# Weight strips taken in pairs: matmuls that alternate between two PSUM banks, instead of 24 in a row into one

## The chip, the cores and the metric

The kernel runs on one core of a Trainium2 chip. The metric is the device time of one execution in microseconds; the shown time is the median of three runs.

## The reference, cut to what matters

Two small networks run one after the other on 512 tokens of width 1024, all in float32. The first has two layers: a state-space mixer with a gated output (`w_glu`), an MLP of 4096, a gated per-layer embedding, then keys and values, sliding-window attention, a second MLP and a second gate. The second has a retention and convolution layer and a latent-attention layer. Nearly all of the work is products of the 512 token columns with weight matrices:

```
ab = y @ w_glu
h = h + jnp.square(jax.nn.relu(hm @ w_up[i])) @ w_down[i]
gate = jax.nn.sigmoid(rmsnorm(h, norm_ple[i]) @ w_ple_gate[i])
hk = rmsnorm(h, kv_norm);  hk @ w_k;  hk @ w_v
mix = swa_sink_attention(q, k_shared, v_shared, attn_sinks[j]) @ w_o[j]
return (o.reshape(b, s, MLA_V) * jax.nn.silu(gate)) @ w_out
```

Each of these lines is a phase (or several) of the common loop that the change touches.

## The kernel before, in words

Tokens lie along the free axis (512 columns), features on the 128 partitions in 8 tiles. Weights arrive as 288 **strips** of 128 x 1024 float32, one strip for each 128 output features with its eight 128x128 blocks (k = 0 to 7). The strips go in one fixed order, the list `PHASES`: `proj0` 2, `glu` 16, the MLP phases `up0_c` and `down0_c` (8 each, eight phases, in the order up 0, up 1, down 0, up 2, down 1, up 3, down 2, down 3), `gate0` 8, `kv` 4, `q` 8, `wo` 8, `proj1` 2, the same MLP phases of layer 1, `gate1` 8, `even` 56, `eout` 16, `odd` 6, `qb` 6, `kvb` 4, `mgate` 8, `oout` 8.

A strip passes four stages, through a ring of `RING = 4` slots:

- SyncE loads it into `raw` (`next_strip`, L394) once the slot's last strip has its low part.
- ScalarE rounds it to `whi` (`split_strip`, L498). It does so for the strip three ahead (`LEAD`) of strip l once `seg_done` says that strip l - 1 is finished, since its slot is then free. `ahead` and `ahead_loop` are these calls, and they stand between ScalarE's other work in program order.
- GpSimd makes the rest `wlo = raw - whi` (`low_strip`, L465) and increments `lo_ready`.
- TensorE multiplies. The token operand too is kept as a high and a low part (`Ah`, `Al` and so on), and a product is three matmuls: whi x high, whi x low, wlo x high (`product`, L831 to L833). So a strip is 8 x 3 = 24 matmuls that accumulate in one PSUM bank; strip l uses bank l modulo 4. Before it starts, `strip` waits for `lo_ready` of the strip and for `evac`, which says that the bank's last result has been read. In the first strip of a phase it also waits for each token tile's `x_lo`.

VectorE and ScalarE read the bank (`evac`), apply the root-mean-square scale, activation or addition, and write the next tiles' high (ScalarE, L521) and low (VectorE, L1375) parts.

`strips` (L933 on) is the common loop: phases without `between` run as a hardware loop of four strips a turn. Five phases (`up0_0`, `gate0`, `kv`, `up1_0`, `gate1`) have `between=norm`: after strip 0 TensorE multiplies the sum of squares with a matrix of ones (`norm`, L949) into another bank, ScalarE takes the root (`root`, L527), VectorE the reciprocal (L1391), and no result of the phase can be read before that. In `mlp` and in the `kv` phase ScalarE's `root` stands ahead of the split of the phase's strip 3 in its program; in `gate` the split of strip 3 stands ahead of `root`, and each later split behind the sigmoid (L637) of one tile.

The phases `proj`, `q`, `even`, `eout`, `odd`, `qb`, `kvb` and `mgate` use other functions (`short_strip`, `strip` alone, `strip_part`) or loops of their own, and stay as they are: 108 of the 288 strips. In `eout` two strips in a row, one from `A` and one from `C`, accumulate into the same bank.

Of the kernel before, what the change touches and what calls it, by code (L numbers as in the profile page):

```python
# [14 lines left out]
P = 128  # L15
TOK = 512
D = 1024
KT = D // P
# [26 lines left out]
RING = 4  # L45
# [14 lines left out]
S0, SEG0, OUT0, NSTR, SEGS = {}, {}, {}, {}, {}  # L60
# [41 lines left out]
class Chain:  # L102
# [14 lines left out]
    def each(self, i, per):  # L117
        self.at, self.first = (i, per), self.n
# [6 lines left out]
def program(nc, a):  # L125

    with ExitStack() as top:
        def sem(name):
            return top.enter_context(nc.semaphore(name))

        def area(stack, name, shape, dt=F32):
            return stack.enter_context(nc.sbuf_tensor(name, shape, dt))


        ps = top.enter_context(nc.psum_tensor("ps", [P, 8, 512], F32))
# [37 lines left out]
        whi = area(main, "whi", [P, RING, D], FR)  # L173
        wlo = area(main, "wlo", [P, RING, D], FR)
        with ExitStack() as p0:
            X = {"P": tuple(area(p0, "P" + part, [P, 2, TOK], FR) for part in "hl")}
# [64 lines left out]
        lo_ready = sem("lo_ready")  # L241
        seg_done = sem("seg_done")
        evac = sem("evac")
        x_hi = sem("x_hi")
        x_lo = sem("x_lo")
# [36 lines left out]
        def C(name):  # L282
            return cst[:, CC[name]]
# [40 lines left out]
        def out_place(sl):  # L324

            return (G if sl // 2 % 2 == 0 else E)[:, sl % 2, :, :]
# [497 lines left out]
        def _(pe):  # L824
            nrm = [0]

            def product(slot, k, bank, xh, xl, first, last):

                w = slice(k * P, (k + 1) * P)
                out = ps[:, bank, :]  # L830
                nc.tensor.matmul(out, whi[:, slot, w], xh, start=first, stop=False)  # L831
                nc.tensor.matmul(out, whi[:, slot, w], xl, start=False, stop=False)  # L832
                return nc.tensor.matmul(out, wlo[:, slot, w], xh, start=False, stop=last)  # L833
# [28 lines left out]
            for k in range(GR // SG):  # L862
                last = nc.tensor.matmul(ps[:, NRM, :], blk[:, :], S[:, k * SG:(k + 1) * SG, :].rearrange("p g c -> p (g c)"),
                                        start=(k == 0), stop=(k == GR // SG - 1))
            last.then_inc(ss_ps, 1)
            transpose_inputs(0)
            for sl in range(NSL):
                pe.wait_ge(c_ready, 1)
                for g in range(SG):
                    gg = sl * SG + g  # L870
                    last = nc.tensor.matmul(ps[:, gg // 32, gg % 32 * GH:(gg % 32 + 1) * GH], E[:, sl % 2, g, :], bC[:, 0, gg * GH:(gg + 1) * GH],
                                            start=True, stop=True)
# [5 lines left out]
                for g in range(SG):  # L878
                    last = nc.tensor.matmul(ps[:, SX, g * NC:(g + 1) * NC], ET[:, g, :], u[:, sl * SG + g, :], start=True, stop=True)
# [3 lines left out]
            for sl in range(NSL):  # L883
# [9 lines left out]
                for g in range(SG):  # L893
                    gg = sl * SG + g
                    nc.tensor.matmul(ps[:, 2 + sl % 2, g * NC:(g + 1) * NC], T[:, gg // (GR // 2), :, gg % (GR // 2)], u[:, gg, :],  # L895
                                     start=True, stop=False)
                    last = nc.tensor.matmul(ps[:, 2 + sl % 2, g * NC:(g + 1) * NC], out_place(sl)[:, g, :], S[:, gg, :],  # L897
                                            start=False, stop=True)
# [5 lines left out]
            def strip(name, l, j, x, xt, step=1, each=None):  # L904

                slot, bank = (S0[name] + j) % RING, (OUT0[name] + j) % RING
                pe.wait_ge(lo_ready, S0[name] + l + 1)
                pe.wait_ge(evac, OUT0[name] + l - RING + 1)
                for k in range(KT):
                    if j == 0:  # L910
                        pe.wait_ge(x_lo, xt + step * k + 1)
                    last = product(slot, k, bank, X[x][0][:, k, :], X[x][1][:, k, :], k == 0, k == KT - 1)
                    if each is not None:
                        each(k)
                last.then_inc(seg_done, 1)

            def strip_part(name, l, part, x):

                slot = (S0[name] + l) % RING
                if part == 0:  # L920
                    pe.wait_ge(lo_ready, S0[name] + l + 1)
                    pe.wait_ge(evac, OUT0[name] + l)
                for k in (2 * part, 2 * part + 1):
                    last = product(slot, k, NRM, X[x][0][:, k, :], X[x][1][:, k, :], k == 0, k == KT - 1)
                if part == 3:
                    last.then_inc(seg_done, 1)
# [6 lines left out]
            def strips(name, x, xt, step=1, n=8, between=None):  # L933

                if between is None:
                    with pe.Fori(0, n // RING) as i:
                        for j in range(RING):
                            strip(name, RING * i + j, j, x, xt, step)
                else:
                    for l in range(n):  # L940
                        strip(name, l, l, x, xt, step)
                        if l == 0:
                            between()

# [6 lines left out]
            def mlp(layer):  # L951
                for kind, c in (("up", 0), ("up", 1), ("down", 0), ("up", 2), ("down", 1), ("up", 3), ("down", 2), ("down", 3)):
                    if kind == "up":
                        strips(f"up{layer}_{c}", "B", XT[f"mlp{layer}"], between=None if c else norm)
                    else:
                        strips(f"down{layer}_{c}", "AC"[c % 2], XT[f"hid{layer}_{c}"])
                strips(f"gate{layer}", "B", XT[f"gate{layer}"], between=norm)
# [25 lines left out]
            for part in range(4):  # L983
                strip_part("q", 1, part, "C")
# [34 lines left out]
            for un in range(U1):  # L1019
                m = un // 4  # L1020
                if m + 2 < KT:
                    strip_part("q", m + 2, un % 4, "C")
                if un % 4 == 0 and m + 1 < KT:
                    pe.wait_ge(rope_done, 3 + m)
                    pe.wait_ge(evac, OUT0["q"] + m + 2)
                    partners(3 + m, "perm1", q1[:, m + 1, :], SZ)
                if un + 3 < U1:
                    scores1(un + 3)
                pe.wait_ge(p_ready, un + 1)
                if un >= 2:  # L1030
                    pe.wait_ge(pt_ready, un - 1)
                for k in range(4):
                    last = nc.tensor.transpose(ps[:, 2 + un % 2, k * P:(k + 1) * P], sm1[:, un % SLOTS, k // 2, k % 2 * P:(k % 2 + 1) * P], C("ident"))
                last.then_inc(pt_ps, 1)
                if un:
                    values1(un - 1)
# [82 lines left out]
            with pe.Fori(0, 2) as i:  # L1119
                for j in range(8):  # L1120
                    slot, bank = (S0["eout"] + j) % RING, (OUT0["eout"] + j // 2) % RING
# [3 lines left out]
                    x, xt = ("A", XT["conv"]) if j % 2 == 0 else ("C", XT["ret"])  # L1125
                    for k in range(KT):
                        if j < 2:
                            pe.wait_ge(x_lo, xt + k + 1)
                        last = product(slot, k, bank, X[x][0][:, k, :], X[x][1][:, k, :], j % 2 == 0 and k == 0, j % 2 == 1 and k == KT - 1)
# [53 lines left out]
            for un in range(U3):  # L1183
                strip_part("mgate", un // 4, un % 4, "A")
                if un + 3 < U3:
                    scores3(un + 3)
                pe.wait_ge(p_ready, U1 + un + 1)
                if un >= 2:
                    pe.wait_ge(pt_ready, U1 + un - 1)
                transposes(sm3[:, un % SLOTS, :], 2 + un % 2, un % NB + 1).then_inc(pt_ps, 1)  # L1190
                if un:
                    values3(un - 1)
# [731 lines left out]
```

## Time and profile before

| | |
|---|---|
| median of 3 runs | 2133.64 us (2131.75 to 2134.81) |
| span of the profiled execution | 2132.1 us |
| TensorE matmuls busy | 1967.1 us (92%), 8728 instructions |
| TensorE weight loads busy | 1578.8 us (74%), 8728 instructions |
| VectorE busy | 982.0 us (46%) |
| ScalarE busy | 730.9 us (34%) |
| GpSimd busy | 880.8 us (41%) |
| load of a strip, 512 KB (288 of them) | 3.6 us from issue to landing |
| chain that ended last | TensorE 80%, VectorE 10%, GpSimd 8%, ScalarE 2% |

The profiled execution stands beside the three runs: its span is 1.5 us under the median. Busy times overlap between engines. The time of one matmul in the profile (some 390 ns) is longer than the step from one matmul to the next, since they are pipelined; the step is what counts. The prologue, to about 240 us, is the state-space mixer.

### The profile page before, as it was taken

The numbers are of one execution on the slowest core, as the hardware profiler recorded it, in microseconds if no ns is written. First come the engines' busy times: TensorE is split into PE (matmuls) and PEld (weight loads), VectorE is DVE, ScalarE is ACT, GpSimd is POOL, SyncE is SP. The second block draws the span as 40 slices with busy tenths as digits, with TensorE's granted clock in tenths as the row PEclk, the third lists the DMA queues.
The fourth block names the chain that finished last, engine by engine and source line by source line (L and its number), as shares of the span: only waits on it lengthen the run. The fifth ranks groups of instructions, "written<-read, shape, count | busy, mean of one in ns | idle before, by whom it ended". The sixth has DMA issues, their size and how long they took to land.

```text
span 2132.1 us, 24312 instructions
## 1 busy us (share of the span) xinstructions
PE 1967.1 (92%) x8728; PEld 1578.8 (74%) x8728; DVE 982.0 (46%) x1425; ACT 730.9 (34%) x1144; POOL 880.8 (41%) x495
## 2 busy tenths in 40 slices
PE   4458999999999899999999999799999999899996
PEld 3457788888888666678888888677877778576674
DVE  7559323212213858843212213844155561467544
ACT  4111434323323534443323323522233332333651
POOL 8995244444444321034444443443433334152121
PEclk8555799999999999999999999899999999899998
DMA  3124433333332220123333332222222223132011
GB/s 136 30 62 117 139 98 92 96 99 99 97 100 89 87 77 23 30 70 94 95 98 99 99 99 89 69 90 79 90 78 79 75 64 109 54 109 60 30 50 40
DMA packets 59298, 175.22 MB, mean 82 GB/s; under 512 B 14784, under 2 KB 15168, under 8 KB 58560
## 3 DMA queue, kind: packets, MB, share of 16 engines
q1 hardware_dynamic: 57344, 170.31, 26.3%
q10 hardware_dynamic: 1872, 3.80, 0.5%
q8 instruction: 54, 0.88, 0.2%
q14 instruction: 28, 0.23, 0.0%
HBM read 163.34 MB, written 4.19 MB: 79 GB/s over the span
## 4 chain that ended last, share of the span: by engine, by line
PE 80%; DVE 10%; POOL 8%; ACT 2%; issue 1%; DMA 0%; DVEq 0%; POOLq 0%
PE ps L831 23%; PE ps L833 22%; PE ps L832 22%; DVE h L1511 1%; PE ps L895 1%; POOL Wc L457 1%; PE ps L1166 1%; PE ps L897 1%; PE ps L964 1%; PE ps L993 1%; POOL G L453 1%; POOL G L454 1%; PE ps L1012 1%; POOL Wsn L458 1%; POOL G L455 1%
## 5 line engine op out<-in xcount | busy, mean ns | idle before, releaser
L465 POOL TENSOR_TENSOR wlo<-raw,whi 128x1024 fp32r<-128x1024 f32 x288 | 715.1, 2485 | 1203.6 <-ACT whi L498 1203.6
L498 ACT ACTIVATE whi<-raw 128x1024 fp32r<-128x1024 f32 x288 | 302.0, 1052 | 391.9 <-PE ps L833 385.5
L831 PE MATMUL ps<-Ch,whi 128*128 128x512 f32 x912 | 365.8, 401 | 13.4 <-DVE Cl L1375 11.3
L833 PE MATMUL ps<-Ch,wlo 128*128 128x512 f32 x912 | 357.3, 392 | 0.0
L832 PE MATMUL ps<-Cl,whi 128*128 128x512 f32 x912 | 357.3, 392 | 0.0
L831 PE MATMUL ps<-Ah,whi 128*128 128x512 f32 x656 | 265.5, 405 | 22.0 <-DVE Al L1375 15.9
L833 PE MATMUL ps<-Ah,wlo 128*128 128x512 f32 x656 | 256.7, 391 | 0.0
L832 PE MATMUL ps<-Al,whi 128*128 128x512 f32 x656 | 256.5, 391 | 0.0
L831 PE MATMUL ps<-Bh,whi 128*128 128x512 f32 x640 | 250.7, 392 | 0.0
L833 PE MATMUL ps<-Bh,wlo 128*128 128x512 f32 x640 | 249.0, 389 | 0.0
L832 PE MATMUL ps<-Bl,whi 128*128 128x512 f32 x640 | 249.0, 389 | 0.0
L831 PEld LDWEIGHTS ps<-Ch,whi 128*128 128x128 f32 x912 | 172.2, 189 | 58.0 <-DVE Cl L1375 13.1
L833 PEld LDWEIGHTS ps<-Ch,wlo 128*128 128x128 f32 x912 | 172.5, 189 | 37.1
L832 PEld LDWEIGHTS ps<-Cl,whi 128*128 128x128 f32 x912 | 172.7, 189 | 35.7 <-issue 1.4
L831 PEld LDWEIGHTS ps<-Ah,whi 128*128 128x128 f32 x656 | 123.9, 189 | 56.0 <-DVE Al L1375 11.9
L832 PEld LDWEIGHTS ps<-Al,whi 128*128 128x128 f32 x656 | 124.1, 189 | 26.5 <-issue 2.7
L833 PEld LDWEIGHTS ps<-Ah,wlo 128*128 128x128 f32 x656 | 123.8, 189 | 26.3
L832 PEld LDWEIGHTS ps<-Bl,whi 128*128 128x128 f32 x640 | 120.1, 188 | 25.8 <-issue 1.0
L831 PEld LDWEIGHTS ps<-Bh,whi 128*128 128x128 f32 x640 | 120.1, 188 | 25.8 <-POOL wlo L465 0.5
L833 PEld LDWEIGHTS ps<-Bh,wlo 128*128 128x128 f32 x640 | 120.1, 188 | 25.1
L1465 DVE TENSOR_TENSOR h<-ps,h 128x512 f32 x48 | 33.2, 692 | 216.4 <-PE ps L833 216.4
L1456 DVE SCALAR_TENSOR_TENSOR ev<-ps,rstd 128x512 f32<-128x512 f32 x64 | 44.3, 691 | 166.6 <-PE ps L833 166.1
(343 smaller groups left out, 2494.5 us busy)
## 6 DMA issues: line engine op xcount, KB each, us to landing
raw<-in_w SPq DMA_DIRECT2D x288, 512.0 KB, 3.6
u<-in_xch SPq DMA_DIRECT2D x1, 2048.0 KB, 12.2
yg<-vsb SPq DMA_DIRECT2D x16, 128.0 KB, 2.3
yg<-z SPq DMA_DIRECT2D x16, 128.0 KB, 2.3
ysc<-yg ACTq DMA_DIRECT2D x8, 256.0 KB, 3.0
h<-in_xfm SPq DMA_DIRECT2D x2, 1024.0 KB, 5.9
out<-h SPq DMA_DIRECT2D x8, 256.0 KB, 2.0
bB<-in_bc SPq DMA_DIRECT2D x1, 1024.0 KB, 7.6
```

What stands on the lines that cost most here:

```text
L453: nc.gpsimd.tensor_tensor(s1, Wc[:, gs, 0:m], w_r, ALU.mult)
L454: nc.gpsimd.tensor_tensor(s2, Wsn[:, gs, 0:m], w_i, ALU.mult)
L455: nc.gpsimd.tensor_tensor(s3, Wc[:, gs, 0:m], w_i, ALU.mult)
L457: nc.gpsimd.tensor_tensor(Wc[:, gs, m:2 * m], s1, s2, ALU.subtract)
L458: last = nc.gpsimd.tensor_tensor(Wsn[:, gs, m:2 * m], s3, s4, ALU.add)
L465: nc.gpsimd.tensor_tensor(wlo[:, r, :], raw[:, r, :], whi[:, r, :].bitcast(F32), ALU.subtract).then_inc(lo_ready, 1)
L498: nc.scalar.activation(whi[:, slot, :], raw[:, slot, :], ACT.Copy).then_inc(hi_ready, 1)
L831: nc.tensor.matmul(out, whi[:, slot, w], xh, start=first, stop=False)
L832: nc.tensor.matmul(out, whi[:, slot, w], xl, start=False, stop=False)
L833: return nc.tensor.matmul(out, wlo[:, slot, w], xh, start=False, stop=last)
L1456: V.scalar_tensor_tensor(ev[:, 0, :], bank(name, j), 0.0, rstd[:, :], ALU.max, ALU.mult).then_inc(evac, 1)
L1465: V.tensor_tensor(h[:, o, :], bank(name, j), h[:, o, :], ALU.add).then_inc(evac, 1)
```

## The change

`strips` takes two strips at a time with the new `two_strips`. For each k it issues six matmuls: whi x high of both strips, whi x low of both, wlo x high of both, so that consecutive matmuls go to two banks in turn. Both banks' results are complete only at the pair's end. The function waits once, ahead of the pair, for `lo_ready` of the second strip and for `evac` of the second bank. `between` runs after the first pair. Nothing is changed on the other engines.

```diff
+            def two_strips(name, l, j, x, xt, step=1):
+
+                slots = [(S0[name] + j + b) % RING for b in range(2)]
+                outs = [ps[:, (OUT0[name] + j + b) % RING, :] for b in range(2)]
+                pe.wait_ge(lo_ready, S0[name] + l + 2)
+                pe.wait_ge(evac, OUT0[name] + l - RING + 2)
+                for k in range(KT):
+                    if j == 0:
+                        pe.wait_ge(x_lo, xt + step * k + 1)
+                    w = slice(k * P, (k + 1) * P)
+                    xh, xl = X[x][0][:, k, :], X[x][1][:, k, :]
+                    for slot, out in zip(slots, outs):
+                        nc.tensor.matmul(out, whi[:, slot, w], xh, start=(k == 0), stop=False)
+                    for slot, out in zip(slots, outs):
+                        nc.tensor.matmul(out, whi[:, slot, w], xl, start=False, stop=False)
+                    for slot, out in zip(slots, outs):
+                        last = nc.tensor.matmul(out, wlo[:, slot, w], xh, start=False, stop=(k == KT - 1))
+                        if k == KT - 1:
+                            last.then_inc(seg_done, 1)
+
...
                 if between is None:
                     with pe.Fori(0, n // RING) as i:
-                        for j in range(RING):
-                            strip(name, RING * i + j, j, x, xt, step)
+                        for j in range(0, RING, 2):
+                            two_strips(name, RING * i + j, j, x, xt, step)
                 else:
-                    for l in range(n):
-                        strip(name, l, l, x, xt, step)
+                    for l in range(0, n, 2):
+                        two_strips(name, l, l, x, xt, step)
                         if l == 0:
                             between()
```

TensorE's order at the start of `glu`, before. `Ah` and `Al` are a token tile's parts, `whi` and `wlo` the strip's, `ps` a bank:

```order
L936 UNCONDITIONAL_BRANCH
L936 ISA
L831 MATMUL ps<-Ah,whi 128x512 [waits x_lo,evac,lo_ready]
L832 MATMUL ps<-Al,whi 128x512
L833 MATMUL ps<-Ah,wlo 128x512
L831 MATMUL ps<-Ah,whi 128x512 [waits x_lo]
```

and now:

```order
L922 REGISTER_ALU [waits lo_ready]
L929 MATMUL ps<-Ah,whi 128x512 [waits x_lo,evac]
L929 MATMUL ps<-Ah,whi 128x512
L931 MATMUL ps<-Al,whi 128x512 x2
L933 MATMUL ps<-Ah,wlo 128x512 x2
L929 MATMUL ps<-Ah,whi 128x512 [waits x_lo]
```

Six matmuls stand between two waits for a token tile, where three did; the number of matmuls and of weight loads is the same.

TensorE's order where the first norm of `up0_0` stands, before:

```order
L831 MATMUL ps<-Bh,whi 128x512 [waits x_lo]
L832 MATMUL ps<-Bl,whi 128x512
L833 MATMUL ps<-Bh,wlo 128x512
L949 MATMUL ps<-acc,cst 128x512 [waits ssq_ready]
L831 MATMUL ps<-Bh,whi 128x512 [waits evac,lo_ready]
L832 MATMUL ps<-Bl,whi 128x512
```

and now:

```order
L929 MATMUL ps<-Bh,whi 128x512 [waits x_lo]
L929 MATMUL ps<-Bh,whi 128x512
L931 MATMUL ps<-Bl,whi 128x512 x2
L933 MATMUL ps<-Bh,wlo 128x512 x2
L969 MATMUL ps<-acc,cst 128x512 [waits ssq_ready]
L929 MATMUL ps<-Bh,whi 128x512 [waits evac,lo_ready]
L929 MATMUL ps<-Bh,whi 128x512
```

The norm (now L969) stands behind 48 matmuls of the phase where it stood behind 24, and the wait behind it is for the low parts of strips 2 and 3, where it was for that of strip 1.

## Rows read from the trace of the kernel before

**Rows 1.** Page, part 2: granted TensorE clock in 40 slices, tenths of full speed
```profile
PEclk8555799999999999999999999899999999899998
```
**Rows 2.** Timeline of PE, the MLP of layer 0; columns: start us, duration us, instruction
```profile
338.64 0.39 PE L832 MATMUL ps<-Bl,whi 128*128 128x512 f32 x1
...
686.39 0.39 PE L833 MATMUL ps<-Bh,wlo 128*128 128x512 f32 x1
```
**Rows 3.** Windows, line L831 alone: stretch, length, PE busy (count), PEld busy, PEclk, DMA share, GB/s
```profile
338.60:686.50 347.90, 199.00 (x512) 95.91 (x511) 1.00 0.32 97
```
**Rows 4.** Timeline of PE, `eout`: first matmul of three strips
```profile
1760.11 0.39 PE L831 MATMUL ps<-Ah,whi 128*128 128x512 f32 x1
...
1765.55 0.39 PE L831 MATMUL ps<-Ch,whi 128*128 128x512 f32 x1
...
1830.83 0.39 PE L831 MATMUL ps<-Ch,whi 128*128 128x512 f32 x1
```
**Rows 5.** Timeline of all engines, first norm of `up0_0`; in brackets idle before and its releaser
```profile
337.56 1.02 PE L949 MATMUL ps<-acc,cst 128*128 128x512 f32 x2
...
338.62 0.69 ACT L527 ACTIVATE std<-ps,cst 128x512 f32<-128x512 f32 x1 [2.20 <-PE ps L949]
...
340.33 2.44 POOL L465 TENSOR_TENSOR wlo<-raw,whi 128x1024 fp32r<-128x1024 f32 x1 [9.81 <-ACT whi L498]
...
342.93 0.69 DVE L1456 SCALAR_TENSOR_TENSOR ev<-ps,rstd 128x512 f32<-128x512 f32 x1 [0.23 <-DVE rstd L1391]
...
348.46 2.65 POOL L465 TENSOR_TENSOR wlo<-raw,whi 128x1024 fp32r<-128x1024 f32 x1 [0.19 <-ACT whi L498]
```
**Rows 6.** Timeline of PE, start of `eout`: matmuls after an idle stretch
```profile
1752.23 0.50 PE L831 MATMUL ps<-Ah,whi 128*128 128x512 f32 x1 [3.30 <-DVE Al L1373]
...
1753.74 0.58 PE L831 MATMUL ps<-Ch,whi 128*128 128x512 f32 x1
...
1756.68 0.63 PE L832 MATMUL ps<-Cl,whi 128*128 128x512 f32 x1
```
**Rows 7.** Timeline of PE, `gate0` from its norm to the norm of `kv`
```profile
686.62 1.02 PE L949 MATMUL ps<-acc,cst 128*128 128x512 f32 x2
...
735.37 0.80 PE L831 MATMUL ps<-Ah,whi 128*128 128x512 f32 x1 [5.34 <-DVE Al L1375]
...
739.57 0.80 PE L831 MATMUL ps<-Ah,whi 128*128 128x512 f32 x1 [2.55 <-DVE Al L1375]
...
741.01 1.91 PE L949 MATMUL ps<-acc,cst 128*128 128x512 f32 x2
```
**Rows 8.** Timeline of all engines, `kv`: low parts of strips 3 and 4, start of `q`
```profile
744.67 4.83 POOL L465 TENSOR_TENSOR wlo<-raw,whi 128x1024 fp32r<-128x1024 f32 x2 [11.45 <-ACT whi L498]
...
759.42 0.39 PE L831 MATMUL ps<-Ch,whi 128*128 128x512 f32 x1
```
**Rows 9.** Timeline of PE, `gate1`: its norm, and the last tile's wait in `even`
```profile
1325.76 1.02 PE L949 MATMUL ps<-acc,cst 128*128 128x512 f32 x2
...
1382.81 0.80 PE L831 MATMUL ps<-Ch,whi 128*128 128x512 f32 x1 [3.08 <-DVE Cl L1375]
```
**Rows 10.** Timeline of PE, strip 0 of `glu`: its start and its last token tile
```profile
240.94 0.39 PE L831 MATMUL ps<-Ah,whi 128*128 128x512 f32 x1
...
249.70 0.50 PE L831 MATMUL ps<-Ah,whi 128*128 128x512 f32 x1 [2.07 <-DVE Al L1426]
```
**Rows 11.** Timeline of DVE, last tile of `wo`, and the first results of `proj1`
```profile
960.58 0.69 DVE L1580 TENSOR_TENSOR h<-ps,h 128x512 f32<-128x512 f32 x1 [2.53 <-PE ps L833]
...
963.41 1.95 DVE L1587 COPY ple<-ps 128x512 f32<-128x512 f32 x3
```
**Rows 12.** Timeline of DVE in `gate1`: making a low part while GpSimd works
```profile
1335.80 2.05 DVE L1375 SCALAR_TENSOR_TENSOR Cl<-h,cols,Ch 128x512 fp32r<-128x512 f32 x1
```
**Rows 13.** Timeline of DVE, last result of `oout`
```profile
2111.09 0.69 DVE L1703 COPY sg<-ps 128x512 f32<-128x512 f32 x1 [3.36 <-PE ps L833]
...
2112.48 0.69 DVE L1385 TENSOR_TENSOR acc<-acc,sq 128x512 f32<-128x512 f32 x1 [0.69 <-ACT sq L762]
```

## The prediction, made before the changed kernel ran

> **What bounds the kernel now.** I read the busy times first, then the clock in the slices, then the timeline of TensorE, then that of all engines around the few places where TensorE waits. TensorE is the bound, and from about a quarter of the span on its clock is granted in full (digits 9) [rows 1]. In the MLP of layer 0 the first and the last of 1,535 matmuls start 347.75 us apart [rows 2]; the window holds 512 of the first of each three, so 64 strips, at clock 1.00 [rows 3]. The step is 347.75 / 1534 = 226.7 ns, a strip 5.44 us. At 2.4 GHz 512 columns are 213.3 ns, so 13.3 ns of each step are something else. The change can gain only if part of that comes from writing one bank again and again.
>
> **Does a change of bank save anything?** Before the change every strip starts in another bank, and `eout` has strips that do not. There an `A` strip and the `C` strip behind it share a bank. From the start of an `A` strip to that of a `C` strip 13 strips later are 70.72 us, 5.440 us each [rows 4], with only six changes of bank among them; the MLP's strips, each with a change, take 24 x 347.75 / 1534 = 5.441 us. Were the step over a change 13.3 ns shorter, the MLP's strips would be 13.3 x 7 / 13 = 7 ns shorter than `eout`'s, and they are not. I take **no gain per matmul**; the bounds are 0 and 13.3 ns for each of the 180 x 24 = 4,320 matmuls in pairs, so 0 to 57.5 us.
>
> The Trainium skill (TensorE: Matmul & The Clock Gate, Back-to-back issue gap) gives columns / 2.4 + 2.5 ns, 216 ns here, where the rows show 226.7; if the alternation brought that step, an estimate from the page's figure is 4,320 x 10.9 ns = 47 us less.
>
> **Steady pairs** cost nothing. A pair is 10.88 us, and when it ends its two slots fall free together, for the pair after the next. The work on two strips in a row is in the trace, since after the norm of `up0_0` two finished strips are caught up on: from the first reading of a bank at 342.93 to the end of the second low part at 348.46 + 2.65 = 351.11 [rows 5] are 8.2 us. With 0.2 us from the pair's end to the first reading, 8.4 of 10.88 us are used; the other 2.5 us cover it. SyncE issues a strip's load when the low part four strips before it is made, so two pairs less 8.4 us, some 13 us, ahead of its split, and it lands in 3.6.
>
> **Start of `glu`: a gain.** Strip 0 starts at 240.94 and waits for tile 7 until 249.70 [rows 10]; with 3 matmuls of it and strip 1 left, two strips end at 249.70 + 0.68 + 5.44 = 255.8. With six matmuls per tile the pair wants tile 7 at 240.94 + 42 x 0.2267 = 250.5, when it is there, and ends at 251.8. **-4.0 us** (0 if the tiles are not what bounds it).
>
> **Norm of `up0_0` and `up1_0`: a new stall.** The norm moves from behind one strip to behind two, and ScalarE's program has the root ahead of the split of strip 3. Now the root runs 1.06 us behind the norm (338.62 - 337.56) and the low part of strip 3 is ready at 340.33 + 2.44 = 342.77, 5.2 us behind it [rows 5]; strip 3 is wanted only at 348.9. After the change the pair (2, 3) is the first thing behind the norm, and the one wait covers both strips: it starts 5.3 us behind the norm where it could have at 0.45. +4.8 us in each. And the clock: after 3.30 us of idle, matmuls from 1753.74 to 1756.68, eight of them, ran at the lower level (1.2 GHz; 2.94 / 7 = 0.42 us a step) [rows 6], 8 x 0.2 = 1.6 us; the bounds are 0 and, from the 5.6 us at `kv` in which the matmuls and the norm were slow (735.37 to 741.01, after 5.34 idle) [rows 7], 13 steps, 2.6 us. Twice **+6.4 us**.
>
> **Norm of `gate0` and `gate1`: the chain behind it starts later.** Both gates are bound by VectorE and ScalarE taking turns on one tile after the other. It starts at the norm, and TensorE, long done with the gate's strips, stands waiting for its last tile: 739.57 in `kv`, 53.0 us behind the norm at 686.62 [rows 7], and 1382.81 in `even`, 57.1 us behind that at 1325.76 [rows 9]. Moved behind a second strip, each norm and its chain come 24 x 0.2267 = 5.4 us later. Pairs (4, 5) and (6, 7) of the gates then also wait for their low parts, which come at the pace of the sigmoids, but TensorE has time in hand: it waited 5.34 + 2.55 us for `kv`'s last two tiles [rows 7], and the pair, with twice the work per tile, uses 4.8 of these. `even` still runs by single strips, so `gate1` costs **+5.4 us**, and `gate0` too.
>
> **`kv`.** Its last tile comes as far behind the norm as before, and strip 1 is by then done but for 3 matmuls, a gain of some 4.8 us. But `kv`'s own norm stands behind the first pair and the low part of strip 3 behind its root: now at 744.67 + 4.83 / 2 = 747.1, 6.1 us behind the norm at 741.01 [rows 7, 8]. The second pair so ends 6.2 + 10.9 + 1.6 (lower clock) = 18.7 us behind it; now `q` starts at 759.42 [rows 8], 18.4 behind it. **+0.3 us** (-1.3 to +1.3).
>
> **`wo` into `proj1`.** The tile round of `wo` is 963.41 - 960.58 = 2.8 us [rows 11]; two of them, 5.7 us, now stand before VectorE reads the first bank of `proj1` (0.7 us more, and 0.2 at the start), whose fifth output wants that bank 5.44 us after `wo` ends: +1.2 us. A low part made while GpSimd worked took 2.05 us [rows 12], where it is 0.75 without; with two or three such meetings it is up to 4.7. I take **+3.0**.
>
> **End of `oout`.** Two results are read after the last matmul instead of one: from copy to sum 2112.48 + 0.69 - 2111.09 = 2.1 us [rows 13]. **+2.0 us**, with nothing to cover it. `wo`, `oout` and `glu` start or end without other waits: their tiles are there.
>
> **Sum:** -4.0 + 6.4 + 5.4 + 0.3 + 3.0 + 6.4 + 5.4 + 2.0 = +24.9 us, on the profiled execution 2132.1 -> 2157.0. Its span is 1.5 us under the median, so the median 2133.64 becomes **2158.5 us** (+1.2%). The bounds of the terms give 2152 to 2167.
>
> **Rivals.**
> - *The alternation speeds every step.* Writing the same bank costs the 13.3 ns, and 4,320 of them vanish: 24.9 - 57.5 = -32.6, 2101 us. For it: the rest above 213.3 ns has no cause in the trace. Against it: the bank changes at every strip and nothing shows there. It is faster than before from 24.9 / 4320 = 5.8 ns a step on.
> - *The stalls are milder.* One gate's delay is taken up, since its strips wait less for each other, and the clock does not fall: about -4 + 2 x 4.8 + 5.4 + 2 = +13, less if the splits come ahead; 2134 to 2147 us.
> - *Pairs hand over late everywhere.* If the second low part came 1 us after it is wanted in the 32 pairs of `up`, +32 us on top, 2190. It decides from 2.5 us of extra work per pair on; the catch-up rows speak against it.
> - *Alternating banks unsettles the clock.* One in ten of the 4,320 steps at 0.42 instead of 0.227 us is +86 us on top, 2245. The clock is 1.00 over 64 strips in four banks in turn [rows 3], which speaks against it.
>
> The Trainium skill (TensorE: Matmul & The Clock Gate, A second HAM failure mode: psum-queue depth-cycling) describes a kernel that cycled through banks and whose clock went up and down for short idles between groups; by that rule, the last rival holds, and this case's trace, which cycles banks already, does not agree.
>
> **How the numbers follow.** My case 0.75; faster steps 0.09; milder 0.09; late pairs 0.05; clock 0.02. The prediction is the first alone, 2158.5. The range 2142 to 2171 holds that case and most of the milder one. A measurement can tell 0.2% (4.3 us) from no change: faster by more than that 0.09, within it 0.03 (the lower end of the milder case), slower 0.88.
>
> **What would show it.** Right: steps of 226.7 ns in the alternating stretches; behind the norms of `up0_0`, `up1_0` and `kv` an idle of 4 to 5 us on TensorE released by GpSimd's low part, then slow matmuls; the last waits of `kv` and `even` still 53 and 57 us behind the norms, with these 10.9 us behind the end of `down`; no wait on TensorE at the start of `glu`; an end with two reads of `oout`. Wrong: a step near 216 ns, or waits on GpSimd inside the MLP at every pair.

## The result, and the profile after

The changed kernel took 2162.11 us (median of four runs, 2161.33 to 2171.18) beside 2133.19 us for the kernel before (2131.75 to 2134.81) on the same chip: a ratio of 1.0144, 95% interval 1.0121 to 1.0166. The forecast was 2158.5 us, with a range of 2142 to 2171. The profiled execution of the change is its slowest, 2171.18 us (span 2169.4, where the other three have 2159.5 to 2160.4); what sets it apart is dealt with in experiment 9, which profiles the same kernel again.

The page of the change, busy times, granted clock and chain of waits:

```profile
PE 1988.1 (92%) x8728; PEld 1592.2 (73%) x8728; DVE 1036.9 (48%) x1425; ACT 728.0 (34%) x1144; POOL 887.7 (41%) x495
...
PEclk8555899999999899898999999989999999899998
...
PE 47%; issue 29%; POOL 16%; DVE 6%; ACT 1%; DMA 0%; SPq 0%; POOLq 0%; DVEq 0%
```

The clock's digits are 8 in four slices where [rows 1] has 9; the second profile of the same kernel, in experiment 9, has 9 in all four, so they are no steady mark of the change. VectorE is busy for 55 us more (982.0 before) with the same 1425 instructions; its operations have become longer, of which more below. Waits of TensorE in the change, all of its engine: us in total, times, longest:

```profile
PE ps L929 <- POOL wlo L465: 20.6, 7, 4.2
...
PE ps L831 <- issue: 5.1, 2, 3.8
```

GpSimd's low parts hold up 7 of the 90 pairs: one in `glu`, one behind each of the norms of `up0_0`, `kv` and `up1_0`, and three inside the gates, where TensorE has time in hand. In the timeline of TensorE the step inside a pair stands in two rows, eight strips apart in the MLP of layer 1:

```profile
1176.09 0.61 PE L929 MATMUL ps<-Ch,whi 128*128 128x512 f32 x2
...
1219.61 0.61 PE L929 MATMUL ps<-Bh,whi 128*128 128x512 f32 x2
```

Eight strips are 192 matmuls; 43.52 / 192 = 226.7 ns, to the digit that of [rows 2]. The alternation of banks gives nothing. The places where the change does something are these, in the same view:

```profile
252.11 0.72 PE L929 MATMUL ps<-Ah,whi 128*128 128x512 f32 x2 [0.23 <-POOL wlo L465]
...
339.26 1.02 PE L969 MATMUL ps<-acc,cst 128*128 128x512 f32 x2
...
344.43 1.22 PE L929 MATMUL ps<-Bh,whi 128*128 128x512 f32 x2 [4.14 <-POOL wlo L465]
...
694.06 1.02 PE L969 MATMUL ps<-acc,cst 128*128 128x512 f32 x2
...
741.79 0.73 PE L929 MATMUL ps<-Ah,whi 128*128 128x512 f32 x2 [0.79 <-DVE Al L1395]
...
745.99 0.73 PE L929 MATMUL ps<-Ah,whi 128*128 128x512 f32 x2 [2.54 <-DVE Al L1395]
...
748.11 1.91 PE L969 MATMUL ps<-acc,cst 128*128 128x512 f32 x2
...
754.17 1.22 PE L929 MATMUL ps<-Ah,whi 128*128 128x512 f32 x2 [4.16 <-POOL wlo L465]
...
983.07 0.76 PE L831 MATMUL ps<-Ch,whi 128*128 128x512 f32 x1 [3.82 <-issue]
...
1007.46 1.22 PE L929 MATMUL ps<-Bh,whi 128*128 128x512 f32 x2 [4.14 <-POOL wlo L465]
...
1358.33 1.02 PE L969 MATMUL ps<-acc,cst 128*128 128x512 f32 x2
...
1415.26 0.79 PE L831 MATMUL ps<-Ch,whi 128*128 128x512 f32 x1 [3.09 <-DVE Cl L1395]
...
2149.55 2.05 PE L969 MATMUL ps<-acc,cst 128*128 128x512 f32 x2 [3.94 <-DVE acc L1405]
```

Read from the top. In `glu` the second pair starts at 252.11; the wait for tile 7 (2.07 us in [rows 10]) is gone. Behind the norm of `up0_0` (339.26) the pair (2, 3) waits until 344.43, 5.2 us, for strip 3's low part, and so at 754.17 in `kv` and 1007.46 in `up1_0`. `gate0`'s norm is at 694.06 and the last tile's wait in `kv` ends at 745.99; there were 52.95 us between these in [rows 7], and are 51.93 now. In layer 1 it is 1415.26 - 1358.33 = 56.93 us, against 57.05 in [rows 9]. At 983.07 stands the idle between `wo` and the fifth output of `proj1`. The final norm waits 3.94 us for the sum of squares; in the trace of before this wait is 2.17.

### The profile page after: what moved, and what is told of

Its sections match the earlier page's. It is cut to its first block, busy times and chain, and to the rows that moved or that the text cites. A ratio compares the mean times of both kernels' runs of the same rounds, so it can differ in the third digit from the quotient of the medians.

```text
span 2169.4 us, 24170 instructions
## 1 busy us (share of the span) xinstructions
PE 1988.1 (92%) x8728; PEld 1592.2 (73%) x8728; DVE 1036.9 (48%) x1425; ACT 728.0 (34%) x1144; POOL 887.7 (41%) x495
## 4 chain that ended last, share of the span: by engine, by line
PE 47%; issue 29%; POOL 16%; DVE 6%; ACT 1%; DMA 0%; SPq 0%; POOLq 0%; DVEq 0%
POOL wlo L465 10%; PE ps L831 8%; PE ps L833 8%; PE ps L832 8%; PE ps L929 6%; PE ps L931 6%; PE ps L933 6%; POOL Wc L457 1%; PE ps L1186 1%; PE ps L984 1%; POOL G L453 1%; POOL G L454 1%; POOL Wsn L458 1%; POOL G L455 1%; POOL G L456 1%
## 5 line engine op out<-in xcount | busy, mean ns | idle before, releaser
L831 PE MATMUL ps<-Ch,whi 128*128 128x512 f32 x592 | 243.4, 411 | 15.9 <-DVE Cl L1395 9.9
L833 PE MATMUL ps<-Ch,wlo 128*128 128x512 f32 x592 | 234.6, 396 | 0.0
L832 PE MATMUL ps<-Cl,whi 128*128 128x512 f32 x592 | 234.5, 396 | 0.0
L929 PE MATMUL ps<-Bh,whi 128*128 128x512 f32 x640 | 201.2, 396 | 16.2 <-POOL wlo L465 16.2
L929 PE MATMUL ps<-Ah,whi 128*128 128x512 f32 x480 | 149.8, 394 | 7.7 <-POOL wlo L465 4.4
L831 PEld LDWEIGHTS ps<-Ch,whi 128*128 128x128 f32 x592 | 113.5, 192 | 48.6 <-issue 13.1
L933 PE MATMUL ps<-Ah,wlo 128*128 128x512 f32 x480 | 149.1, 392 | 0.0
L931 PE MATMUL ps<-Al,whi 128*128 128x512 f32 x480 | 149.0, 392 | 0.0
L833 PEld LDWEIGHTS ps<-Ch,wlo 128*128 128x128 f32 x592 | 113.5, 192 | 24.9
L832 PEld LDWEIGHTS ps<-Cl,whi 128*128 128x128 f32 x592 | 113.8, 192 | 23.7 <-issue 1.4
```

Source lines behind the costliest of these rows:

```text
L929: nc.tensor.matmul(out, whi[:, slot, w], xh, start=(k == 0), stop=False)
L933: last = nc.tensor.matmul(out, wlo[:, slot, w], xh, start=False, stop=(k == KT - 1))
```

## The experiments

Two theories stood. Mine: the loss is at the seams (norms, gates, `wo` into `proj1`, the end), and pairing itself is free. The rival: alternation costs something everywhere, in the step, the clock or the handing over. Each ratio below is to the kernel before, run beside the experiment on the same chip.

**1. The norm behind one strip again.** In the phases with a norm, strip 0 goes alone, then the norm, strip 1 alone, then pairs.

```diff
-                    for l in range(0, n, 2):
+                    strip(name, 0, 0, x, xt, step)
+                    between()
+                    strip(name, 1, 1, x, xt, step)
+                    for l in range(2, n, 2):
                         two_strips(name, l, l, x, xt, step)
-                        if l == 0:
-                            between()
```

> The change, but in the five phases with a norm the first two strips run singly with the norm between them, as before the change; all other strips stay in pairs. Theory (the cost is the place of the norm): the stalls behind the norms and the later start of the gate chains go, by the deltas read between the profiles about 5.7 + 7.0 (MLPs) + 5.1 + 5.3 (gates) + 1.6 (kv) = 24.7 us, so 2162 - 25 = 2137 us (2134 to 2142). Rival (pairs cost at every hand-over, wherever the norm stands): 2155 us or more. Rival (alternating banks is itself slower): over 2155 too.

Measured: 2151.22 us (2150.24 to 2152.64), ratio to before 1.0079 [1.0062, 1.0095]. The direction is right and the size is not, by 14 us. The five norms had not been all of it. Two rows of its timeline of TensorE show a piece that I had not thought of, at the start of `gate0`:

```profile
683.77 0.50 PE L831 MATMUL ps<-Bh,whi 128*128 128x512 f32 x1 [1.07 <-DVE Bl L1396]
...
686.59 1.97 PE L970 MATMUL ps<-acc,cst 128*128 128x512 f32 x2 [1.84 <-DVE acc L1406]
```

`down0_3` still ends with a pair, so its last two tiles come out together: strip 0 of the gate waits for one, and the norm behind it for the sum of both. These waits and the clock behind them are 3.35 us ahead of each gate, 6.7 in all. The norm behind a pair hides them. Another 3.1 us stay inside the gates: from their norms to the last tile are 54.63 and 58.47 us, where the kernel before has 52.95 and 57.05, and pairs in them still wait for low parts (1.62 and 1.41 us). The 3.85 us in front of `proj1`'s fifth output and the longer end stayed as well. So a pair costs something at its *end* too, wherever the next phase wants its last tile.

**2. Three matmuls to a bank, then three to the other.** The change with its inner loops merged: per k whi x high, whi x low, wlo x high of the one strip, then of the other. The pairs are the same, the bank changes at each third matmul instead of at each.

```diff
                     for slot, out in zip(slots, outs):
                         nc.tensor.matmul(out, whi[:, slot, w], xh, start=(k == 0), stop=False)
-                    for slot, out in zip(slots, outs):
                         nc.tensor.matmul(out, whi[:, slot, w], xl, start=False, stop=False)
-                    for slot, out in zip(slots, outs):
                         last = nc.tensor.matmul(out, wlo[:, slot, w], xh, start=False, stop=(k == KT - 1))
```

> The change with the same pairs and waits, but three matmuls in a row into one bank, then three into the other. Theory (the bank plays no part in the step): step 226.7 ns in the MLP, 2162 us within 3 us. Rival (a change of bank at every matmul costs or saves something): with a third of the changes, 4,320 x 2/3 steps differ; a saving or cost of 5 ns each would move the time by 14 us, either way.

Measured: 2163.21 us (2160.01 to 2166.07), ratio 1.0134 [1.0117, 1.0150]: the change's own time. In the timeline of TensorE the same eight strips of the MLP take the same 43.52 us, so 226.7 ns a step:

```profile
1176.01 0.39 PE L929 MATMUL ps<-Ch,whi 128*128 128x512 f32 x1
...
1219.53 0.39 PE L929 MATMUL ps<-Bh,whi 128*128 128x512 f32 x1
```

How often the bank changes does not matter. What the change costs comes from the pairing of strips.

**3. Pairs in `glu` only.** The kernel before, with `two_strips` in that one phase.

```diff
+                if name == "glu":
+                    with pe.Fori(0, n // RING) as i:
+                        for j in range(0, RING, 2):
+                            two_strips(name, RING * i + j, j, x, xt, step)
```

> The kernel before with pairs in glu alone. Theory (six matmuls per token tile cover the late tiles): 3.7 us less than before, 2129.5 us (2128 to 2131), and no wait for tiles in the first pair of glu. Rival (the gain in glu came from the step or is lost again behind it): 2133 us.

Measured: 2130.54 us (2129.75 to 2132.41), ratio 0.9983 [0.9974, 0.9993]: faster, by less than 0.2%. The profiles say it more sharply: every marker from the first norm to the last (335.01 against 337.56, 2109.80 against 2113.23) lies 2.6 to 3.6 us earlier. The first norm gains the least, since `up0_0`'s strip 0 now waits for the last tile of `glu`, which comes out of a pair; the kernel before has no such wait:

```profile
334.21 0.50 PE L831 MATMUL ps<-Bh,whi 128*128 128x512 f32 x1 [0.90 <-DVE Bl L1399]
```

Where a phase's tiles come one by one and late, a pair does useful work in the gaps.

**4. `wo` by single strips,** the rest as in the change.

```diff
+                        if name == "wo":
+                            for j in range(RING):
+                                strip(name, RING * i + j, j, x, xt, step)
+                        else:
+                            for j in range(0, RING, 2):
+                                two_strips(name, RING * i + j, j, x, xt, step)
```

> The change with single strips in wo. Theory (two last tiles of wo stand ahead of the first reading of proj1, each longer while GpSimd works, and the clock falls in the stall): the 7.1 us between the start of proj1 and the start of up1_0 go, 2162 - 7 = 2155 us (2153 to 2158), and proj1 takes 10.9 us again. Rival (the stall is proj1's low parts coming late, whatever wo does): 2162 us.

Measured: 2158.39 us, but 2152.26 to 2166.21, ratio 1.0121 [1.0090, 1.0153]; the median alone decides nothing. The profile does: from `proj1`'s first matmul to the first of `up1_0` are 10.9 us as before the change, where the change has 17.8, and the idle of 3.8 us is gone. The seam belongs to `wo`'s last pair.

**5. The split of strip 3 ahead of the root.** In ScalarE's program for `up0_0`, `up1_0` and `kv`, the split of the phase's strip 3 is put in front of the square root, as `gate` has it.

```diff
+                ahead(f"up{layer}_0", 0)
                 root(D)
...
+                    if kind == "up" and c == 0:
+                        dst = X["A"][0]
+                        for o in range(8):
+                            if o:
+                                ahead(name, o)
...
+            ahead("kv", 0)
             root(D)
```

> The change with one thing moved on ScalarE: the split of strip 3 of up0_0, up1_0 and kv stands ahead of the root instead of behind it; the norm stays behind the first pair. Theory (TensorE's stall behind these norms is the wait for that strip's low part): the three idle stretches of 4.1 us released by GpSimd behind norms of up0_0, up1_0 and kv go, and the slow matmuls behind them; from the first norm to that of gate0 349 us instead of 355; in all 3 x 4.1 to 3 x 6 = 12 to 18 us less, 2144 to 2150 us. Rival (the later norm itself delays the MLP, through the readings of the banks): a wait on VectorE takes the place of the wait on GpSimd, 2158 us or more.

Measured: 2149.50 us (2146.72 to 2153.70), ratio 1.0085 [1.0070, 1.0101], so 12.6 us less than the change. Behind the norm of `up0_0` TensorE goes on at once, at full clock, and meets a smaller wait one pair later:

```profile
338.55 1.02 PE L980 MATMUL ps<-acc,cst 128*128 128x512 f32 x2
339.01 1.02 PE L940 MATMUL ps<-Bh,whi 128*128 128x512 f32 x2
...
352.11 0.73 PE L940 MATMUL ps<-Bh,whi 128*128 128x512 f32 x2 [1.61 <-POOL wlo L465]
```

The stall behind the norms was made by the order of ScalarE's program, and not by a lack of time on GpSimd: the same low parts in another order cost `up0_0` 1.9 us instead of 5.7 to 6.0.

**6. Pairs only where the tiles come late.** The kernel before, with pairs in all of `glu`, in strips 0 and 1 of `kv`, of `even` and of `odd`, and the split of `kv`'s strip 3 ahead of the root, as in experiment 5.

```diff
+                elif name == "kv":
+                    two_strips(name, 0, 0, x, xt, step)
+                    between()
+                    for l in range(2, n):
+                        strip(name, l, l, x, xt, step)
...
+            two_strips("even", 0, 0, "C", XT["even"])
+            norm()
+            norm(acc2, SX)
...
+            two_strips("odd", 0, 0, "A", XT["odd"], each=add_squares)
```

> The kernel before with pairs only where TensorE waits for the token tiles of the preceding phase: all of glu, and strips 0 and 1 of kv, even and odd; the norm of kv's split order as in e5 (split ahead of root). Theory (the second strip fills the waits, and nothing else in the pairs helps): glu -3.5, kv -4.8 or a little less, even -5 to -6, odd -4 to -5, together 2134 - 18 = 2116 us (2113 to 2121). Rival (the norms of even and odd come no earlier, because VectorE's work on the tile chain sets them, so the filled time only becomes a later wait): 2126 us or more.

Measured: 2120.71 us (2119.08 to 2123.06), ratio 0.9946 [0.9933, 0.9960]: faster than both kernels. The timeline of TensorE at its three new pairs, and at a wait behind the second:

```profile
734.86 1.22 PE L930 MATMUL ps<-Ah,whi 128*128 128x512 f32 x2 [2.54 <-DVE Al L1408]
...
1372.20 0.73 PE L930 MATMUL ps<-Ch,whi 128*128 128x512 f32 x2 [2.20 <-DVE Cl L1408]
...
1390.45 0.47 PE L832 MATMUL ps<-Ch,whi 128*128 128x512 f32 x1 [2.33 <-DVE q L1429]
...
1832.99 1.19 PE L930 MATMUL ps<-Ah,whi 128*128 128x512 f32 x2 [7.82 <-DVE Al L1408]
```

`kv` had waits of 5.34 and 2.55 us [rows 7] and has 0.44 and 2.54; q's partner products (the matmuls of `partners` with which the attention begins) start 9.83 us earlier than before, 3.7 of them from `glu`. In `even` waits of 3.08, 5.11 and 3.08 became one of 4.36 ahead of the pair, for its low parts, and one of 2.20, and the norm behind them gained 6.8 us. By 1390.45, 1.2 of these were lost again: 1.0 because the norm's matmuls now run at the lower clock (2.3 us for the four, 1.3 before), 0.2 in the wait for VectorE at 1390.45, which was 2.13 us before. In `odd` the 7.82 us are a wait for the *first* tile, as in the kernel before, and the pair gains nothing.

**7. Single strips at the seams only.** The change, but the first two strips of the five norm phases, and the last two of `down0_3`, `down1_3`, `wo` and `oout`, go alone; about nine tenths of the paired strips still alternate.

```diff
-                if between is None:
+                if between is None and name not in ("down0_3", "down1_3", "wo", "oout"):
...
+                elif between is None:
+                    for l in range(0, n - 2, 2):
+                        two_strips(name, l, l, x, xt, step)
+                    for l in (n - 2, n - 1):
+                        strip(name, l, l, x, xt, step)
```

> The change with single strips at every seam: the first two strips of the five phases with a norm, and the last two of down0_3, down1_3, wo and oout; the other strips in pairs, the alternation in about nine of ten of the strips kept. Theory (all of the cost is at seams): 3.4 us gained in glu remain, some 1.7 in kv and up to 4 from the clock in the attention are lost, 2131 to 2138 us. Rival (pairs inside the phases cost too): over 2142 us.

Measured: 2136.89 us (2134.62 to 2138.25), ratio 1.0020 [1.0011, 1.0030]. With nine seams changed back, 25 of the 29 us are gone, although 162 strips still go in pairs. This settles it against the rival. The median is still 4.0 us over the kernel before, with the gain in `glu` inside. Its profile shows two kinds of wait that single strips at the seams do not take away:

```profile
683.85 1.12 PE L975 MATMUL ps<-acc,cst 128*128 128x512 f32 x2 [1.07 <-DVE acc L1411]
...
964.10 0.47 PE L831 MATMUL ps<-Ch,whi 128*128 128x512 f32 x1 [1.73 <-issue]
```

From norm to norm each MLP takes 1.2 us longer than before, most of it the wait for the sum of squares at the gate, and `proj1` 2.0 us (12.9 instead of 10.9). Another 1.9 us lie between the last tile in `even` and the last norm; of the phases there only `oout` is paired, and it takes as long as before.

**8. As 6, without the pair in `odd`.**

```diff
-            two_strips("odd", 0, 0, "A", XT["odd"], each=add_squares)
-            for l in range(2, NSTR["odd"]):
+            for l in range(NSTR["odd"]):
+                strip("odd", l, l, "A", XT["odd"], each=None if l else add_squares)
```

> The kernel before with pairs in glu and at the start of kv and even, and no pair in odd. In the experiment that paired odd too, the first pair of odd began behind a wait of 7.8 us for its first tile, as the single strip did, and no tile after it was waited for; the offset against before went from -15.3 us at the norm ahead of odd to -14.1 us at the next norm. Theory: a pair gains only where its tiles come later than TensorE takes them, so odd gained nothing: span of the profiled execution 2117 to 2118.5, median 2119 to 2121, the offset at the last norm -14.5 to -16. Rival: the odd pair did gain and the loss came from elsewhere: 2 us or more slower than with it, median over 2122.5.

Measured: 2119.07 us (2116.84 to 2123.69), ratio 0.9939 [0.9924, 0.9955]; span of the profile 2117.0, last norm 15.1 us ahead of before (14.0 in experiment 6). The pair in `odd` gave nothing, as the theory says; this is the fastest version, though within scatter of the sixth.

**9. The change once more, unedited,** for a profile that is not its slowest run.

> The changed kernel as it is, once more, for a profile that is not the slowest of its runs. Median 2160 to 2163, span of the profile some 2160. Theory: the 4.6 us that its first profile lost in the attention (lower granted clock in its last 16 us) are by chance of that run: here the offset against before changes by -1 to +1 us between the start of q's partner products and the start of wo; the offsets elsewhere are as before within 0.5 us: glu -3.7, up0_0 +5.7, gate0 +5.1, wo into proj1 +7, up1_0 +7, gate1 +5.3, end +1.8. Rival: the attention's loss belongs to the change: again +4 us or more there.

Measured: 2162.08 us (2161.67 to 2165.35), ratio 1.0142 [1.0124, 1.0160], profiled execution 2161.67, span 2159.9. The windows of the attention's last part, of the change's first profile and then of this one (length, busy times with counts, clock, DMA share, GB/s):

```profile
889.00:930.00 41.00, 38.07 (x175) 26.31 (x175) 28.92 (x79) 19.20 (x58) 2.41 (x1) 0.79 0.05 14
```

```profile
889.00:925.00 36.00, 31.04 (x175) 21.76 (x174) 29.65 (x81) 21.12 (x59) 2.41 (x1) 1.00 0.06 16
```

The same matmuls, at a granted clock of 0.79 and of 1.00. From the start of q's partner products to `wo` the first profile lost 4.6 us on before; this one gained 0.8. The same kernel does both, so the pairs do not always bring this loss. Whether they make it likelier stays open: of the eight profiles with pairs in most phases (the change twice, experiments 1, 2, 4, 5, 7 and 10) four lose 3.1 to 4.7 us there, and of the four with few or none (before, experiments 3, 6 and 8) none does. The other offsets hold only in part: `gate0` came out at +3.4 instead of +5.1, `wo` into `proj1` at +5.7 instead of +6.9.

**10. A later split at the seam of `wo`.** The change, where ScalarE waits for the first result of `proj1` to be read before it splits the strips ahead.

```diff
+            act.wait_ge(evac, OUT0["proj1"] + 1)
             for l in range(2):
                 ahead("proj1", l)
```

> The changed kernel; ScalarE waits until VectorE has read the first result of proj1 before it splits the strips two and three ahead, so that GpSimd makes no low part while VectorE works on the last two tiles of wo. In the change's traces a low part of wo's last tile took 1.6 us and the sum behind it 2.84 to 2.88 us (GpSimd at work), where they are 0.75 and 0.69 us before. Theory: GpSimd's work stretches these; without it VectorE reads the banks of proj1 some 3 us sooner, TensorE's idle before proj1's fifth output falls from 3.8 to 0.5 to 1.5 us, its slow matmuls behind it vanish or shrink to a few; proj1 takes 11.5 to 13 us instead of 16.6 to 17.8; median 2156 to 2159. Rival: the stretched operations are VectorE's own (two tile rounds back to back), and the idle stays over 3 us; median 2160 to 2164. If the later low parts hold up the first pairs of up1_0, an idle released by GpSimd's low part shows at the start of up1_0.

Measured: 2159.14 us (2158.05 to 2165.52), ratio 1.0119 [1.0102, 1.0136]. The interval overlaps that of the change, so the time alone does not decide it; the profiles do. First the timeline of all engines at the end of `wo` in the change (profile of experiment 9):

```profile
971.75 5.21 POOL L465 TENSOR_TENSOR wlo<-raw,whi 128x1024 fp32r<-128x1024 f32 x2 [0.40 <-ACT whi L498]
...
971.83 2.88 DVE L1405 TENSOR_TENSOR acc<-acc,sq 128x512 f32<-128x512 f32 x1
...
974.63 2.47 DVE L1607 COPY ple<-ps 128x512 f32<-128x512 f32 x4
...
975.40 0.47 PE L831 MATMUL ps<-Ch,whi 128*128 128x512 f32 x1 [3.84 <-issue]
```

and in this experiment:

```profile
983.88 0.68 DVE L1406 TENSOR_TENSOR acc<-acc,sq 128x512 f32<-128x512 f32 x1
984.49 3.12 DVE L1608 COPY ple<-ps 128x512 f32<-128x512 f32 x5
...
985.27 0.47 PE L832 MATMUL ps<-Ch,whi 128*128 128x512 f32 x1 [1.64 <-issue]
...
986.34 4.80 POOL L465 TENSOR_TENSOR wlo<-raw,whi 128x1024 fp32r<-128x1024 f32 x2 [2.93 <-ACT whi L498]
```

The sum of squares takes 0.68 us without a low part beside it, 2.88 with one: it starts at 971.83, 0.08 us behind the low part. TensorE's idle falls from 3.84 to 1.64 us, no slow matmul follows, and `proj1` takes 12.8 us instead of 16.6 (10.9 before the change). The theory holds for the stretched operations; the idle is a little over the 1.5 us that I gave as its most. `up1_0` starts without a wait for a low part, so the later splits cost nothing.

The Trainium skill (SBUF — State Buffer, Who interferes with whom) states that a VectorE instruction with two SBUF inputs and a GpSimd instruction that reads SBUF block each other whole, and that the one that starts first keeps the port. By that rule, the trace agrees: the addition, with both inputs in SBUF, lasts until the first of the two low parts (5.21 / 2 = 2.6 us each) has ended, and the copies from PSUM at 974.63 run at 0.6 us each beside the second.

## Why the prediction was right, and where its terms were not

The time lay 3.6 us over the forecast, in the range, and in the main for the reasons given: the dense stream gains nothing, and the seams pay. That the sum comes within 3 us of the second profile's is in part luck, since `wo` (2.7 too low) and `even` (1.7 where nothing was forecast) are offset by `gate0` (2.0 too high) and the attention (0.8). The terms, from marker to marker against the kernel before (`up0_0` to `up0_0` and so on, the two profiles of the change):

| | forecast | first profile | second profile |
|---|---|---|---|
| start of `glu` | -4.0 | -3.7 | -3.7 |
| `up0_0` | +6.4 | +5.7 | +6.0 |
| `gate0` to the norm of `kv` | +5.4 | +5.1 | +3.4 |
| `kv` to q's partner products | +0.3 | +1.6 | +0.7 |
| attention | 0 | +4.6 | -0.8 |
| `wo` into `proj1` | +3.0 | +6.9 | +5.7 |
| `up1_0` | +6.4 | +7.0 | +6.6 |
| `gate1` to the last tile in `even` | +5.4 | +5.3 | +5.4 |
| `even` to the last norm, without the end | 0 | +2.1 | +1.7 |
| end of `oout` | +2.0 | +2.7 | +2.8 |
| sum | +24.9 | +37.3 | +27.8 |

- **No gain per matmul**: right. The step is 226.7 ns in pairs, and experiment 2 shows that the number of bank changes has no part in the time. The estimate of 47 us less, from the Trainium skill's figure for the gap of an isolated matmul (TensorE: Matmul & The Clock Gate, Back-to-back issue gap), is not borne out: the step stayed 10.9 ns over it in both orders.
- **Steady pairs**: right. In the change no pair inside an MLP waits for GpSimd but the one right behind the norm; in experiment 5 it is the pair after that one, 1.6 us in each MLP.
- **Start of `glu`**: right, and shown alone by experiment 3. The prediction had no wait at the *end* of `glu`; experiment 3 shows one of 0.90 us, which in the change falls away, since the pair of `up0_0` has other work meanwhile.
- **Norms of `up0_0` and `up1_0`**: right, with the place, the releaser and the slow matmuls behind it (an idle of 4.14 us, then steps at 1.2 GHz). Experiment 5 shows the cause.
- **Gates**: right for `gate1`, within 0.1 us. In `gate0` the chain from its norm to the last tile is 1 to 2 us shorter than in [rows 7]. That is no effect of the pairs that these profiles can show: six profiles of this same paired `gate0` (the change twice, experiments 2, 4, 5 and 10) read 50.9 to 53.6 us, and experiment 3, whose `gate0` is as before, reads 52.0, against 52.95 before. What makes it differ between executions stays open. Experiment 1 adds what the prediction did not see: moving the norm back does not win the 5.4 us in full, since the sum of squares of a pair's tiles is late.
- **`wo` into `proj1`**: the mis-sized term. The prediction bounded a stall between 1.2 and 4.7 us and took 3.0. The stall was 3.82 us and lay within these bounds, nearer to the upper, since VectorE's sum met a low part as in [rows 12] and worse (2.88 us). What was left out is the clock: behind 3.30 us of idle the rows of before show slow matmuls [rows 6], the text charged for it at the norms, and did not at this stall. It was worth 3.1 us in the first profile (14 slow matmuls behind the idle) and 1.9 in the second (8). With the idle as measured and the clock as charged at the norms, the sum would have been 3.8 + 1.6 = 5.4 us.
- **`even` to the last norm**: put at nothing, and measured at +2.1 and +1.7. Of its phases only `oout` is paired, and it takes as long as before. 1.6 us arise inside `even`, between the wait for VectorE at 1406.71 and the next wait, at 1483.28: 76.57 us before, 78.19 in both profiles of the change. The windows of this stretch, before and in the change's first profile, differ in the granted clock (the figure behind the five busy times):

```profile
1407.00:1484.00 77.00, 76.23 (x338) 60.26 (x337) 36.45 (x48) 15.23 (x19) 28.09 (x12) 1.00 0.27 89
```

```profile
1439.00:1518.00 79.00, 78.23 (x339) 61.72 (x338) 36.02 (x47) 16.03 (x20) 27.67 (x12) 0.98 0.28 86
```

The pairs are not the cause: the stretch takes 76.6 us in experiments 1, 3, 5, 6 and 10 and 78.2 in 2, 4, 7 and 8, and the kernels of 6 and 8 are the same up to `odd`, which comes later.

- **End of `oout`**: 1.8 us of longer wait as forecast (3.94 - 2.17), and 1.0 us more behind the last norm, whose two matmuls then take 2.05 us instead of 1.12: again the clock behind an idle.
- **Rivals.** Faster steps: refuted by the step of 226.7 ns in the change, and again by experiment 2. Late pairs everywhere and an unsettled clock: refuted by experiment 7. The milder case is refuted by the rows above: both gates paid, and the clock did fall. The Trainium skill's account of a kernel that cycles through banks, with short idles between its groups of matmuls and a clock that swings (TensorE: Matmul & The Clock Gate, A second HAM failure mode: psum-queue depth-cycling), is borne out here for the idles and not for the banks: through the paired MLPs, from a few us behind the norm on, TensorE does not idle and the steps stay at 226.7 ns, and behind the first norm slow matmuls stand only after waits and in the attention, which is full of short ones.

## What to carry to other kernels

Pair independent accumulations where their common input arrives piece by piece and late, and nowhere else: there a pair fills gaps (0.5 to 0.6% here, with one split of ScalarE moved), while in a stream that is already dense it gains nothing and delays everything at its ends, from the norm behind its first strip to the reader of its last. When the unit of work is doubled, go through each seam and ask what the next engine does in program order before it makes the *second* unit ready; the cheapest repair is often to reorder that engine's program (12.6 us from moving three splits). And charge the clock at every new long idle of TensorE (here those of 3.8 and 4.1 us were followed by slow matmuls, the one of 1.64 was not, and one of 2.1 us in `even` was in some executions only), not only at those that come to mind first.

## What the runs showed of the hardware

- A VectorE addition with both inputs in SBUF that starts just behind a low part of GpSimd (2.4 to 2.6 us) takes 2.88 us instead of 0.68, and a VectorE low part that starts in the middle of one takes 1.6 instead of 0.75; moving GpSimd's work away restores the addition (experiment 10). VectorE's busy time rose by 55 us under the change with the same number of instructions; more than half of that, 29 us, are the 69 additions into `acc` (48.7 us before, 78.0 in the change).
- The attention of the same kernel ran at a granted clock of 0.79 in one execution and 1.00 in another over its last 36 to 41 us, a difference of some 5 us between runs of one kernel. A stretch of `even` takes 76.6 or 78.2 us in kernels that are the same up to its end (experiments 6 and 8). An effect of a few us in a part with short gaps can't be read from a single profile.
- The step is 226.7 ns whether the bank changes with every matmul, with every third, or with every 24th.
